# A ninth place for key rows, and turned value indices made one quarter earlier, in a one-core decoder layer with a product-key expert mixer

## Chip, cores and metric

One core of one Trainium2 chip. The metric is the device time of one launch in microseconds (us), the median of several runs. "Faster" and "slower" are against the kernel before, measured on the same chip.

## What is computed

One inference step of one decoder layer, for a prompt of 512 tokens and 8 sample tokens that share all parameters, model width 1024, everything in float32. The dense part is a recurrent branch beside a windowed attention branch, a gated merge and an output product. Then comes the expert mixer, and it is here that the change lies:

```python
def peer(h, w_pq, sub_keys, u_tab, v_tab):
    ...
    s = jnp.einsum('nhsd,hskd->nhsk', q.astype(jnp.float32), sub_keys.astype(jnp.float32))
    sv, si = lax.top_k(s, PEER_TOPK)
    cand = (sv[:, :, 0, :, None] + sv[:, :, 1, None, :]).reshape(n, PEER_HEADS, PEER_TOPK * PEER_TOPK)
    ...
    fv, fp = lax.top_k(cand, PEER_TOPK)
    ...
    def chunk(args):
        hc, ec, gc = args
        u = jnp.take(u_tab, ec, axis=0)
        act = jax.nn.gelu(jnp.einsum('cd,ced->ce', hc, u).astype(jnp.float32), approximate=False)
        wgt = (gc * act).astype(hc.dtype)
        vr = jnp.take(v_tab, ec, axis=0)
        return jnp.einsum('ce,ced->cd', wgt, vr)
```

Each token has 8 heads with 16 chosen experts each, so 128 rows of `u_tab` and 128 rows of `v_tab`, 4 KB each. A residual sum and a last norm follow.

## The kernel before

Five engines run programs of their own and meet at semaphores. The dense part goes in two chunks: tokens 0 to 255, then 256 to 511 with the 8 samples. It is a list of numbered products (`_plan`, `NO`), each with an estimated cost (`COST`), which TensorE works off in order into five PSUM buffers; the other engines follow its numbers.

The expert part of the first chunk can begin when its first scores are there (product 171, `PEER_FROM`), at about 383 us. From then on all engines interleave it with the rest of the dense list, step by step. A step is called a **quarter**. `MIDDLE[k]` and `LIMITS[k]` say how many dense products every engine has behind it in the middle and at the end of quarter k; the dense list is used up at quarter 140. There are 65 **groups** of 8 experts for 128 tokens (16 for each tile of 128 tokens, and group 48 for the 8 samples), so 520 slots on either side.

What a group goes through:

- **Key rows.** GpSimd gathers `u_tab` rows, one indirect DMA of 128 rows (512 KB) for each slot, two slots a quarter (`gather_u`, L2087; all gathers are recorded at L2085). Slot n goes to place n mod 8 of `u_row`. It waits for `s_idx` (the head's indices) and, from group 1 on, for `s_urd`, the dot that last read this place.
- **Dots.** VectorE multiplies the gathered row by the token's row and sums, one instruction (and the read of its sum) for each slot, two a quarter, two quarters behind (`dot_products`, L1910; the dot is L1924). Each lets `s_urd` go up.
- **Weights.** ScalarE makes gelu(dot) times the softmax share, in quarter 4g + 6 (`weights`, L1426; L1439, L1442).
- **Pack, turn and copy.** The value rows are wanted in another layout, 32 tokens for each row of partitions, so the indices and weights of a group have to be moved across partitions. VectorE packs them (`turn` on VectorE, L1993; L2000, waits for the group's weights `s_wcol`), TensorE turns them into the PSUM buffer `turned` (`turn` on TensorE, L1100; L1111, L1112, waits for `s_apart`), ScalarE copies the indices to `vidx` (L1460) and the weights to `spread` (L1461). `V_FROM[g]` is the quarter in which the first value row of group g is gathered. Before the change the pack stands in quarter `V_FROM[g] - 3`, the turn in `V_FROM[g] - 2` and the copy in `V_FROM[g] - 1`.
- **Value rows.** GpSimd gathers `v_tab` rows into the 8 places of `vt_row` (`gather_v`, L2100), between the key rows and in the same in-order queue. From quarter 11 to 127 these are three in two quarters, then some 2.4 a quarter (`V_AT`). A value gather waits for `s_vidx` and for the sums that last read its place (`s_vrd`). Groups 62 and 64 use the places of the key rows, since those are free at the end (`IN_U_PLACE`).
- **Sums.** TensorE multiplies `spread` by the value rows into the PSUM tensor `y`, four slots at a time, two quarters behind (`expert_sums`, L1115; L1128, 16 products). When a tile is complete the residual and the norm follow.

The order within a quarter on TensorE is: dense up to `MIDDLE`, the sums that are due, dense up to `LIMITS`, then a turn if one is due:

```python
                if k < len(LIMITS):
                    course.until(LIMITS[k])
                if k + TURN_LEAD - 1 in V_FROM and k + TURN_LEAD - 1 != V_FROM[SAMPLE_GROUP]:
                    turn(V_FROM.index(k + TURN_LEAD - 1))
```

Weights of the dense products come through SP's own DMA queue, and share the 16 DMA engines with the gathers.

## Time and profile before

| | us |
|---|---|
| median of 3 runs | 2036.07 |
| the runs | 2042.62, 2036.07, 2018.65 |
| the profiled execution | 2039.13 |
| its span | 2036.7 |
| busy: TensorE products, VectorE, ScalarE, GpSimd | 1348.9, 1282.7, 555.3, 1148.0 |
| moved by DMA | 701.81 MB, 545.33 of it by the gathers |

The profile is of one execution. In it a busy time is the sum over an engine's instructions. An idle time in brackets stands before the instruction named, with the one whose end let it go; a semaphore is counted by what raised it. "issue" means that the engine waited for nothing that the profile shows. Each row of a gather is the time in which GpSimd writes its descriptors; the transfer comes after it.

### The profile page before, as it was taken

The numbers are of one execution on the slowest core, as the hardware profiler recorded it, in microseconds if no ns is written. First come the engines' busy times: TensorE is split into PE (matmuls) and PEld (weight loads), VectorE is DVE, ScalarE is ACT, GpSimd is POOL, SyncE is SP. The second block draws the span as 40 slices with busy tenths as digits, with TensorE's granted clock in tenths as the row PEclk, the third lists the DMA queues.
The fourth block names the chain that finished last, engine by engine and source line by source line (L and its number), as shares of the span: only waits on it lengthen the run. The fifth ranks groups of instructions, "written<-read, shape, count | busy, mean of one in ns | idle before, by whom it ended". The sixth has DMA issues, their size and how long they took to land.

```text
span 2036.7 us, 23255 instructions
## 1 busy us (share of the span) xinstructions
PE 1348.9 (66%) x7318; PEld 870.6 (43%) x7318; DVE 1282.7 (63%) x3168; ACT 555.3 (27%) x1518; POOL 1148.0 (56%) x1062
## 2 busy tenths in 40 slices
PE   6998999748787787889878775343443344444344
PEld 5887899636555555666555442110111111111111
DVE  3265345577888888766767656566666556665640
ACT  2446423132354245112213222112112112211110
POOL 0100100356665556657666767777777777777774
PEclk9999999969889888879989887566666656666667
DMA  9755345799999988999999999999999999999997
GB/s 363 262 172 201 114 156 196 272 346 368 403 348 383 357 306 323 401 380 377 409 406 410 409 406 390 381 374 379 390 405 366 376 375 391 325 408 381 382 404 291
DMA packets 202440, 701.81 MB, mean 345 GB/s; under 512 B 22568, under 2 KB 32368, under 8 KB 202032
## 3 DMA queue, kind: packets, MB, share of 16 engines
q0 software_dynamic: 149760, 545.33, 69.3%
q1 hardware_dynamic: 52560, 155.02, 21.1%
q8 instruction: 59, 0.97, 0.2%
q14 instruction: 61, 0.50, 0.1%
HBM read 691.26 MB, written 11.06 MB: 345 GB/s over the span
## 4 chain that ended last, share of the span: by engine, by line
PE 25%; DMA 18%; issue 18%; DVE 17%; POOL 17%; ACT 3%; POOLq 0%; SPq 0%; DVEq 0%; ACTq 0%
POOL arena L2085 17%; DMA arena<-in_v_tab,pku 13%; PE acc L775 8%; DVE arena L1924 6%; PE y L1128 6%; DMA arena<-in_u_tab,pku 4%; PE acc L833 2%; PE acc L787 2%; PE acc L788 2%; PE acc L789 2%; ACT arena L1222 1%; DVE arena L1661 1%; PE acc L802 1%; DMA arena<-w_mod 1%; DVE pku L1945 1%
## 5 line engine op out<-in xcount | busy, mean ns | idle before, releaser
L1924 DVE CUSTOM_DVE_ANT_0 arena<-arena 128x1024 f32<-128x1024 f32 x520 | 627.2, 1223 | 368.7 <-DMA arena<-in_u_tab,pku 359.9
L2085 POOL DMA_INDIRECT arena<-in_u_tab,pku x520 | 567.4, 1091 | 400.3 <-issue 151.8
L1128 PE MATMUL y<-arena 128*32 128x512 f32 x2080 | 414.3, 909 | 548.3 <-DMA arena<-in_v_tab,pku 548.3
L2085 POOL DMA_INDIRECT arena<-in_v_tab,pku x520 | 565.5, 1088 | 232.3 <-issue 149.1
L775 PE MATMUL acc<-arena 128*128 128x264 f32 (+1 forms) x2304 | 544.0, 394 | 16.2 <-ACT arena L1238 7.6
L775 PEld LDWEIGHTS acc<-arena 128*128 128x128 f32 x2304 | 443.1, 195 | 120.9 <-issue 49.1
L1128 PEld LDWEIGHTS y<-arena 128*32 128x32 f32 x2080 | 82.4, 143 | 778.9 <-issue 768.7
L1460 ACT CAST pku<-turned 128x8 uint32<-128x8 f32 x64 | 10.2, 160 | 371.8 <-PE turned L1112 371.8
L1442 ACT ACTIVATE pk<-pk 128x1 f32<-128x1 f32 x520 | 103.5, 281 | 2.1
L1111 PE MATMUL turned<-arena 128*128 128x256 f32 x128 | 58.3, 547 | 59.3 <-DVE arena L2000 59.2
L2127 POOL TENSOR_TENSOR o_lo<-arena,o_hi 128x256 fp32r<-128x256 f32 x8 | 6.6, 866 | 156.7 <-ACT o_hi L1341 156.7
L1439 ACT ACT_TABLE_LOAD x37 | 47.5, 1283 | 157.9 <-issue 102.3
L1111 PEld LDWEIGHTS turned<-arena 128*128 128x128 f32 x128 | 26.6, 252 | 129.7 <-DVE arena L2000 64.7
L1439 ACT ACTIVATE pk<-pk 128x8 f32<-128x8 f32 x65 | 13.6, 209 | 198.0 <-DVE pk L1924 184.5
L1247 ACT ACTIVATE arena<-acc 128x256 f32<-128x256 f32 (+1 forms) x32 | 12.4, 386 | 152.6 <-PE acc L775 90.4
L833 PE MATMUL acc<-arena 128*128 128x256 f32 (+1 forms) x208 | 49.5, 396 | 5.6 <-DVE arena L1630 5.6
L1573 DVE SCALAR_TENSOR_TENSOR arena<-arena,par 128x256 f32<-128x256 f32 x60 | 29.1, 485 | 34.0 <-ACT arena L1281 32.6
L1741 DVE TENSOR_TENSOR w_lo<-arena,w_hi 128x1024 fp32r<-128x1024 f32 x32 | 39.1, 1228 | 14.4 <-ACT w_hi L1181 13.2
L1733 DVE SCALAR_TENSOR_TENSOR arena<-arena,acc 128x256 f32<-128x256 f32 (+1 forms) x16 | 6.8, 425 | 64.5 <-PE acc L775 64.5
L833 PEld LDWEIGHTS acc<-arena 128*128 128x128 f32 x208 | 39.9, 195 | 15.5 <-issue 9.5
L2117 POOL MEMSET arena<- 128x1536 f32 x2 | 2.8, 1388 | 76.6 <-DVEq L1784 76.6
L1222 ACT ACTIVATE arena<-arena,stat 128x256 f32<-128x256 f32 x64 | 31.7, 496 | 51.0 <-DVE stat L1667 51.0
(246 smaller groups left out, 1834.0 us busy)
## 6 DMA issues: line engine op xcount, KB each, us to landing
arena<-w_mod SPq DMA_DIRECT2D x48, 512.0 KB, 5.7
arena<-w_pq SPq DMA_DIRECT2D x32, 512.0 KB, 6.9
arena<-w_xr SPq DMA_DIRECT2D x20, 512.0 KB, 8.7
arena<-w_qk SPq DMA_DIRECT2D x20, 512.0 KB, 7.2
arena<-w_gr SPq DMA_DIRECT2D x20, 512.0 KB, 7.0
arena<-w_rnn SPq DMA_DIRECT2D x16, 640.0 KB, 6.3
arena<-in_u_tab,pku POOLq DMA_INDIRECT x520, 7.3
arena<-in_v_tab,pku POOLq DMA_INDIRECT x520, 6.7
```

The source lines that it names most:

```text
L775: mm = pe.matmul(a[:, 0:n], w[:, k, :], rhs[:, k, 0:n], start=(k == 0), stop=(k == ks - 1))
L787: pe.matmul(a[:, 0:CP], w1[:, k, :], hi[:, k, :], start=(k == 0), stop=False)
L788: pe.matmul(a[:, 0:CP], w1[:, k, :], lo[:, k, :], start=False, stop=False)
L789: mm = pe.matmul(a[:, 0:CP], w2[:, k, :], hi[:, k, :], start=False, stop=(k == DC - 1))
L833: mm = pe.matmul(a[:, 0:n], w[:, gate, i, :], xc[:, k, 0:n], start=(i == 0), stop=(i == len(BAND[j]) - 1))
L1111: pe.matmul(turned[:, 0:SLOT * 32], apart[n % 2][:, P:2 * P], to_rows, start=True, stop=True)
L1128: mm = pe.matmul(y[rows, h, :], spread[g % NTURN][:, 32 * j:32 * j + 32], rows_v[j][:, h * 512:(h + 1) * 512], start=first and (g != SAMPL ...
L1222: act.activation(probs[i % 2][:, j, :], probs[i % 2][:, j, :], ACT.Exp, bias=st[:, j:j + 1], accum_out=st[:, G + j:G + j + 1])
L1439: act.activation(gl, dots[g % 2], ACT.Gelu).then_inc(s_gl, 1)
L1442: ins = act.activation(wcol[at][:, j:j + 1], gl[:, j:j + 1], ACT.Copy, scale=gains[:, j:j + 1])
L1924: dve.tensor_tensor_reduce(u_row[j], u_row[j], h_of[o], 1.0, 0.0, ALU.mult, ALU.add, dots[g % 2][:, j:j + 1]).then_inc(s_urd, 1)
L2085: pool.indirect_dma_start(out=row, out_offset=None, in_=table, in_offset=bass.IndirectOffsetOnAxis(ap=idx, axis=0), **more).then_inc(signa ...
```

## The change

Two things.

The key rows get a ninth place. `u_row` and its semaphores `s_u` have 9 entries, slot n goes to place n mod 9, and a key gather waits for the dot of the ninth slot before it, no longer of the eighth. The areas behind it in the arena move by 4 KB for each partition. Value groups 62 and 64 still use key places 0 to 7, and count the fills of each by the new numbers.

`TURN_LEAD` goes from 3 to 4: the pack stands four quarters ahead of the group's first value gather, the turn three and the copy two.

```diff
+UPLACES = 9
...
-DOTS_LAG, TURN_LEAD, SUMS_LAG = 2, 3, 2
+DOTS_LAG, TURN_LEAD, SUMS_LAG = 2, 4, 2
...
+U_FILLS = [len(range(j, U_SLOTS, UPLACES)) for j in range(SLOT)]
+U_LAST = [range(j, U_SLOTS, UPLACES)[-1] for j in range(SLOT)]
...
-        u_row = [area(A_U + j * D, D) for j in range(SLOT)]
+        u_row = [area(A_U + j * D, D) for j in range(UPLACES)]
...
-                    pe.wait_ge(landed[j], 16 * V_NTH[g])
+                    pe.wait_ge(landed[j], 16 * (V_NTH[g] + (U_FILLS[j] if g in IN_U_PLACE else 0)))
...
-                    dve.wait_ge(s_u[j], 16 * (g + 1))
-                    dve.tensor_tensor_reduce(u_row[j], u_row[j], h_of[o], 1.0, 0.0, ALU.mult, ALU.add,
+                    nth, place = divmod(SLOT * g + j, UPLACES)
+                    dve.wait_ge(s_u[place], 16 * (nth + 1))
+                    dve.tensor_tensor_reduce(u_row[place], u_row[place], h_of[o], 1.0, 0.0, ALU.mult, ALU.add,
...
-                if g:
-                    pool.wait_ge(s_urd, SLOT * (g - 1) + j + 1)
+                n = SLOT * g + j
+                if n >= UPLACES:
+                    pool.wait_ge(s_urd, n - UPLACES + 1)
...
                 elif V_BEFORE[g] is None:
-                    pool.wait_ge(s_urd, SLOT * GROUPS + j + 1)
+                    pool.wait_ge(s_urd, U_LAST[j] + 1)
```

Line numbers of the changed kernel are 5 to 7 higher from here on (TensorE's products L775, L1111, L1112 and L1128 are L780, L1116, L1117 and L1133 there; VectorE's L1924 and L2000 are L1930 and L2006; GpSimd's L2085 is L2091).

GpSimd, the start of the gathers, with the semaphores waited for (`s_idx` indices of a head, `s_urd` dots, `s_ready` a dense product, `s_vidx` turned indices). Before:

```order
L2085 DMA arena<-in_u_tab,pku 128x1024 [waits s_idx]
L2085 DMA arena<-in_u_tab,pku 128x1024 x7
L2085 DMA arena<-in_u_tab,pku 128x1024 [waits s_idx,s_urd]
L2085 DMA arena<-in_u_tab,pku 128x1024 [waits s_urd] x7
L2085 DMA arena<-in_u_tab,pku 128x1024 [waits s_idx,s_urd]
L2085 DMA arena<-in_u_tab,pku 128x1024 [waits s_urd] x6
```
Changed:

```order
L2091 DMA arena<-in_u_tab,pku 128x1024 [waits s_idx]
L2091 DMA arena<-in_u_tab,pku 128x1024 x7
L2091 DMA arena<-in_u_tab,pku 128x1024 [waits s_idx]
L2091 DMA arena<-in_u_tab,pku 128x1024 [waits s_urd] x7
L2091 DMA arena<-in_u_tab,pku 128x1024 [waits s_idx,s_urd]
L2091 DMA arena<-in_u_tab,pku 128x1024 [waits s_urd] x6
```
The ninth gather waits no longer for a dot; the order is the same.

TensorE at the value rows that are first gathered in quarter 86 (group 14; `turned` is its turn, `y` the sums of others, `acc` dense products). Before:

```order
L1128 MATMUL y<-arena 32x512 x8
L775 MATMUL acc<-arena 128x264 x10
L915 MATMUL acc<-arena 64x2 x32
L917 MATMUL acc<-arena 64x64
L915 MATMUL acc<-arena 64x2 x32
L917 MATMUL acc<-arena 64x64
L775 MATMUL acc<-arena 128x264 x8
L1128 MATMUL y<-arena 32x512 x8
L1111 MATMUL turned<-arena 128x256
L1112 MATMUL turned<-arena 128x8
```
Changed:

```order
L1133 MATMUL y<-arena 32x512 x8
L780 MATMUL acc<-arena 128x264 x10
L920 MATMUL acc<-arena 64x2 x32
L922 MATMUL acc<-arena 64x64
L920 MATMUL acc<-arena 64x2 x32
L922 MATMUL acc<-arena 64x64
L1116 MATMUL turned<-arena 128x256
L1117 MATMUL turned<-arena 128x8
L780 MATMUL acc<-arena 128x264 x8
L1133 MATMUL y<-arena 32x512 x8
```
The turn stands ahead of 8 dense products and of a set of sums, behind which it stood before.

VectorE at the pack of the same group (L2000 before, L2006 in the changed one; MAX, MAX_INDEX and MATCH_REPLACE belong to the ranking of a later head, ISA is a dot). Before:

```order
L1952 TENSOR_TENSOR arena<-pk 128x256
L1956 MAX pk<-arena 128x8
L1957 MAX_INDEX pku<-pk,arena 128x8
L1959 MATCH_REPLACE arena<-pk,arena 128x256
L1956 MAX pk<-arena 128x8
L1957 MAX_INDEX pku<-pk,arena 128x8
L1960 TENSOR_SCALAR pk<-pk 128x1
L2000 TENSOR_TENSOR arena<-pk,arena 128x256
L1723 COPY arena<-acc 128x64
L1724 TENSOR_TENSOR arena<-arena,acc 128x64
L1726 COPY arena<-arena 128x8x8
L1924 ISA arena,pk<-arena 128x1024
```
Changed:

```order
L1953 MATCH_REPLACE arena<-pk,arena 128x128
L1950 MAX pk<-arena 128x8
L1951 MAX_INDEX pku<-pk,arena 128x8
L1954 CAST pk<-pku 128x32
L2006 TENSOR_TENSOR arena<-pk,arena 128x256
L1738 SCALAR_TENSOR_TENSOR arena<-arena,acc 128x264
L1930 ISA arena,pk<-arena 128x1024
L1930 ISA pk 128x1
L1930 ISA arena,pk<-arena 128x1024
L1930 ISA pk 128x1
L1958 TENSOR_TENSOR arena<-pk 128x256
L1962 MAX pk<-arena 128x8
```
The pack has moved ahead of a dense operation, two dots and the second ranking.

TensorE at the end of its program, the last turn. Before:

```order
L1112 MATMUL turned<-arena 128x8
L1128 MATMUL y<-arena 32x512 x16
L1111 MATMUL turned<-arena 128x256
L1112 MATMUL turned<-arena 128x8
L1128 MATMUL y<-arena 32x512 x16
L1111 MATMUL turned<-arena 128x256
L1112 MATMUL turned<-arena 128x8
L1128 MATMUL y<-arena 32x512 x32
```
Changed:

```order
L1117 MATMUL turned<-arena 128x8
L1133 MATMUL y<-arena 32x512 x16
L1116 MATMUL turned<-arena 128x256
L1117 MATMUL turned<-arena 128x8
L1133 MATMUL y<-arena 32x512 x16
L1116 MATMUL turned<-arena 128x256
L1117 MATMUL turned<-arena 128x8
L1133 MATMUL y<-arena 32x512 x40
```
The last turn has 8 more products of the sums behind it.

## Rows read from the trace of the kernel before

**Rows 1.** The page: busy share of the 16 DMA engines and rate, in 40 slices.

```profile
DMA  9755345799999988999999999999999999999997
GB/s 363 262 172 201 114 156 196 272 346 368 403 348 383 357 306 323 401 380 377 409 406 410 409 406 390 381 374 379 390 405 366 376 375 391 325 408 381 382 404 291
```

**Rows 2.** Busy time by stretch: us, each engine's busy us (instructions), PEclk, DMA share, GB/s.

```profile
400.00:820.00 420.00, 307.03 (x1412) 214.78 (x1416) 348.90 (x910) 161.63 (x441) 248.92 (x222) 0.85 0.94 355
820.00:1240.00 420.00, 341.33 (x1770) 239.83 (x1762) 286.73 (x719) 102.74 (x306) 277.93 (x251) 0.89 1.01 400
900.00:920.00 20.00, 20.00 (x131) 16.45 (x131) 8.88 (x25) 2.51 (x6) 6.25 (x7) 0.71 0.79 285
1250.00:1970.00 720.00, 299.21 (x1272) 83.05 (x1272) 439.66 (x1036) 124.44 (x419) 552.58 (x517) 0.61 0.99 381
```

**Rows 3.** Timeline, GpSimd: start, us, line, operation, idle before it and releaser.

```profile
383.01 1.09 POOL L2085 DMA_INDIRECT arena<-in_u_tab,pku  x1 [130.93 <-DVE pku L1983]
...
1453.75 1.27 POOL L2085 DMA_INDIRECT arena<-in_v_tab,pku  x1 [0.30 <-issue]
...
2018.10 0.94 POOL L2085 DMA_INDIRECT arena<-in_v_tab,pku  x1 [0.30 <-issue]
```

**Rows 4.** The page, costliest groups: the gathers of key and value rows.

```profile
L2085 POOL DMA_INDIRECT arena<-in_u_tab,pku x520 | 567.4, 1091 | 400.3 <-issue 151.8
L2085 POOL DMA_INDIRECT arena<-in_v_tab,pku x520 | 565.5, 1088 | 232.3 <-issue 149.1
```

**Rows 5.** Waits of GpSimd, 400 to 1250 us: us in total, times, longest.

```profile
POOL arena L2085 <- DVE pk L1924: 106.5, 37, 7.7
POOL arena L2085 <- PE y L1128: 38.5, 14, 7.7
POOL arena L2085 <- ACT pku L1460: 18.5, 5, 5.5
POOL arena L2085 <- DVE pku L1983: 13.2, 2, 7.1
```

**Rows 6.** Waits of GpSimd, 1250 to 1970 us.

```profile
POOL arena L2085 <- PE y L1128: 13.8, 17, 4.8
POOL arena L2085 <- ACT pku L1460: 2.7, 9, 0.3
POOL arena L2085 <- DVE pk L1924: 1.8, 1, 1.8
```

**Rows 7.** Timeline: GpSimd behind a dot, then TensorE behind value rows, twice.

```profile
570.39 1.61 POOL L2085 DMA_INDIRECT arena<-in_u_tab,pku  x1 [6.77 <-DVE pk L1924]
...
594.37 3.49 PE L1128 MATMUL y<-arena 128*32 128x512 f32 x16 [9.44 <-DMA arena<-in_v_tab,pku]
...
820.32 1.14 POOL L2085 DMA_INDIRECT arena<-in_u_tab,pku  x1 [2.50 <-DVE pk L1924]
...
838.90 3.64 PE L1128 MATMUL y<-arena 128*32 128x512 f32 x16 [4.34 <-DMA arena<-in_v_tab,pku]
```

**Rows 8.** Waits of TensorE for value rows: 400 to 820 us, then 820 to 1250 us.

```profile
PE y L1128 <- DMA arena<-in_v_tab,pku: 21.8, 4, 9.4
...
PE y L1128 <- DMA arena<-in_v_tab,pku: 76.2, 17, 9.9
```

**Rows 9.** Timeline, 901 to 918 us: pack, turn, and the gathers that waited.

```profile
901.77 0.42 DVE L2000 TENSOR_TENSOR arena<-pk,arena 128x256 f32<-128x256 f32 x1
...
910.41 1.14 POOL L2085 DMA_INDIRECT arena<-in_u_tab,pku  x1 [6.72 <-DVE pk L1924]
...
915.20 0.70 PE L1111 MATMUL turned<-arena 128*128 128x256 f32 x2
...
917.09 0.93 POOL L2085 DMA_INDIRECT arena<-in_v_tab,pku  x1 [5.54 <-ACT pku L1460]
```

**Rows 10.** Timeline, GpSimd, the last 50 us: gathers that waited for indices.

```profile
1998.47 0.94 POOL L2085 DMA_INDIRECT arena<-in_v_tab,pku  x1 [1.42 <-ACT pku L1460]
...
2009.39 0.94 POOL L2085 DMA_INDIRECT arena<-in_v_tab,pku  x1 [1.28 <-ACT pku L1460]
```

More of the change, by code:

```diff
@@ L320 @@
 V_BEFORE = [max([e for e in range(g) if (e in IN_U_PLACE) == (g in IN_U_PLACE)], default=None) for g in range(GROUPS + 1)]
-V_NTH = [sum(1 for e in range(g + 1) if (e in IN_U_PLACE) == (g in IN_U_PLACE)) + (GROUPS + 1 if g in IN_U_PLACE else 0) for g in range(GROUPS + 1)]
+V_NTH = [sum(1 for e in range(g + 1) if (e in IN_U_PLACE) == (g in IN_U_PLACE)) for g in range(GROUPS + 1)]
+U_FILLS = [len(range(j, U_SLOTS, UPLACES)) for j in range(SLOT)]
+U_LAST = [range(j, U_SLOTS, UPLACES)[-1] for j in range(SLOT)]
 A_H = 0
@@ L330 @@
 A_U = A_RING + OWN * SLOTW
-A_V = A_U + SLOT * D
+A_V = A_U + UPLACES * D
 A_HCUR = A_V + SLOT * D
@@ L502, in peer_program @@
         s_sidx, s_idxread = sem("s_sidx"), sem("s_idxread")
-        s_u = [sem(f"s_u{j}") for j in range(SLOT)]
+        s_u = [sem(f"s_u{j}") for j in range(UPLACES)]
         s_vt = [sem(f"s_vt{j}") for j in range(SLOT)]
@@ L2094, in gather_u @@
                         pool.wait_ge(s_idx, head + 1)
-                if g:
-                    pool.wait_ge(s_urd, SLOT * (g - 1) + j + 1)
+                n = SLOT * g + j
+                if n >= UPLACES:
+                    pool.wait_ge(s_urd, n - UPLACES + 1)
                 idx = eidx[head % NINDEX][:, part * SLOT + j:part * SLOT + j + 1] if g != SAMPLE_GROUP else eidx_s[:, j:j + 1]
-                gather(u_row[j], X["u_tab"], idx, s_u[j], {"engine_sem": s_idxread} if part and j == SLOT - 1 else {})
+                gather(u_row[n % UPLACES], X["u_tab"], idx, s_u[n % UPLACES], {"engine_sem": s_idxread} if part and j == SLOT - 1 else {})
             def gather_v(g, j):
```

## The prediction

> **What bounds the kernel now.** Read the 40 slices first [rows 1]. From the ninth slice on the DMA digit is 9 in all but three, so the first impression is a kernel held by its transfers. The rate row beside it says more: from there on the best slices stand at 401 to 410 GB/s, the others at 291 to 391. So 409 is about what the transfers can do here, and a slice below it is one in which less was asked for, or in which the asking was slow.
>
> The table by stretch [rows 2] divides the gathers' time. From 400 to 820 us VectorE is busy for 348.9 of 420 us (83%) and the rate is 355 GB/s: dense work on VectorE sets the pace. From 820 to 1240 us the rate is 400 GB/s and TensorE and the transfers set it together. From 1250 to 1970 us there is no dense work; VectorE is busy for 61% of it, TensorE for 42%, the rate is 381.
>
> Then GpSimd, which issues all 1040 gathers in one fixed order. A gather that meets nothing takes 0.94 us, with 0.30 us before it [rows 3]. From the first at 383.01 to the last at 2018.10 are 1635.1 us. At 1.24 us each, 1039 steps are 1288.4. The two groups of gathers are busy for 567.4 + 565.5 = 1132.9 us [rows 4], which is 155.3 over 1040 x 0.94. What is left, 1635.1 - 1288.4 - 155.3 = 191.4 us, is waiting. From 400 to 1250 us that is 106.5 us for dots (37 times), 38.5 for sums, 18.5 for turned indices, 13.2 for new indices [rows 5]. From 1250 to 1970 us only 1.8, 13.8 and 2.7 us are put down to dots, sums and indices, mostly the bare 0.30 [rows 6]. So the second half is an unbroken row of issues (517 gathers in 720 us, 1.39 us each), the first half is a chain of waits in which GpSimd stands before a full set of key places. The change works on the waits of the first half; the end moves only by as much as GpSimd reaches the second half earlier, and by what the last 50 us give.
>
> **The ninth place.** It removes no instruction and adds none: 520 dots, 520 key gathers, 520 value gathers as before, in the same order on GpSimd; only the dot waited for is the ninth before, not the eighth. Two dots fall in a quarter. Rows 2 have 222 + 251 = 473 gathers in 840 us, at mostly 3.5 a quarter, so a quarter is about 6.2 us and a dot comes every 3.1 us. The mean wait for a dot is 106.5 / 37 - 0.30 = 2.6 us. So one place more covers the average wait once. It does not cover it 37 times: where VectorE sets the pace, GpSimd runs one gather further ahead and then stands before the tenth. The sum of waits falls only as far as the pace itself gets quicker, or where a stretch of waiting is followed by one in which GpSimd or the transfers are late. So I do not book the 106.5 us. I book the places where TensorE waits for value rows that stood behind a GpSimd waiting for a dot. There are two clear ones before 850 us [rows 7]: GpSimd waits 6.77 us until 570.39 and TensorE then 9.44 us until 594.37; GpSimd waits 2.50 us until 820.32 and TensorE 4.34 until 838.90. The first value gather is also held by a value place, so I take 3 of its 6.5 us, and 2.2 of the other: 5 us. Below, nothing (VectorE is 83% busy there); above, the 21.8 us that TensorE waits for value rows in it [rows 8].
>
> **Indices one quarter earlier.** Each group's pack on VectorE, turn on TensorE and copy on ScalarE move by one quarter, in all 64 groups (the samples' group has only ScalarE's part); nothing is added. Their distance to each other stays one quarter, so where TensorE waits for a pack it comes to it a quarter earlier and is let go a quarter earlier, and I book nothing. What ends are GpSimd's waits for indices. The clearest is at 917.09 us, 5.54 us, right after one of 6.72 for a dot at 910.41; the turn that it waited for stood at 915.20 on TensorE behind a product and a sum set, although its pack was ready at 901.77 [rows 9]. With the turn in front of that product and that sum set, as the order shows, the indices are there before 910. In this hole the rate was 285 GB/s from 900 to 920 [rows 2]; at 409 those 20 us need 14, so the hole is worth 6.1 us, and both halves of the change work on it. I take 5; at least 0, at most 12.0 (both waits less 0.30 each). The waits of this kind left are in a queue already at 409 and I count them as nothing: the transfers there come when they come.
>
> In the last 50 us the case is plain. After the last key gather the value gathers follow at 1.24 us, and TensorE and ScalarE turn indices just in time: 1.42 us before 1998.47 and 1.28 before 2009.39 [rows 10], less 0.30 each, is 2.1 us, on the path that ends the run. Now the last turn stands 8 products earlier. The cover is the 8 places; I book all 2.1.
>
> **What it may cost.** The pack waits for its group's weights. For group 0 it had two quarters after them and has one; for later groups two or more. Behind it on VectorE stand dots, for which GpSimd and ScalarE wait. One such wait would be at most a quarter, 6 us, once; I take 0. The ninth place also puts a further 512 KB ahead of what SP and GpSimd ask for later, priced below as a rival.
> Gathers that no longer wait for the end of a dot will now issue beside one. Rows show what that is worth: the mean gather is 0.15 us over the bare 0.94, a single one among many dots 1.27 [rows 3, 4]; 37 x 0.15 = 6 us of GpSimd's time, in a stretch where it waits for some 160, so 0.
> On this the Trainium skill is harsher (SBUF — State Buffer, "SBUF: two separate sides"): a VectorE operation with two SBUF inputs and a GpSimd operation that reads SBUF exclude each other for the whole instruction. By that rule each of the 37 could lose a whole dot, and half the gain of the ninth place would go. The trace agrees in that long gathers are there at all and that the last one, when the dots have ended, takes 0.94 [rows 3]; it does not show a dot's whole length on average.
>
> **The sum.** 5 + 5 + 2.1 = 12.1 us. The profiled execution took 2039.1 (span 2036.7), 3.1 over the median of 2036.1 of the runs shown. 2039.1 - 12.1 = 2027.0, and against the median 2024.0.
>
> **Rivals.**
> First, the waits were a symptom. Where VectorE or the transfers set the pace, GpSimd merely changes the place at which it waits. For it: 83% VectorE, 400 GB/s in the second stretch, and from 1250 us on next to no waits for dots [rows 6], so that a further place has nothing to do there. Against it: the hole at 900. It leaves the tail's 2.1: 2034.
> The skill has a rule that would make this the only case (DMA: Bandwidth & Descriptors, "Specifications"): a core's limit to HBM is about 358 GB/s. By it the 381 and 400 GB/s of the stretches would be past the limit and no earlier gather could gain. The trace contradicts it with slices of 410, so it gets no more chance than the rows give.
> Second, the holes close. At 409 GB/s the bytes of the first stretch need 420 x 355/409 = 364.5 us, those of the second 410.8: 64.7 us below what they take. VectorE's 348.9 busy us would just allow it. But one place is one gather, and more than a third of that would surprise me: 22 + 2.1 = 24, so 2012.
> Third, slower. In the queue at 409 one more gather ahead is one more transfer of 512 KB, 1.28 us, before the value rows that TensorE waits for. From 820 to 1250 us TensorE waits for them 17 times, 76.2 us in all [rows 8]; 17 x 1.28 (524,288 bytes at 409 GB/s) = 22 us, if the dense products behind those waits carry it to the end. It decides if key rows are asked for before they are needed while value rows are late, which is what a place on the key side alone does. Against it: the number of gathers is the same, so the further one is ahead only once, and GpSimd asks for the value rows earlier as well. 2034 + 22 = 2056.
> That the change does not do what it says can only be in part: the order shows the ninth gather without its wait and the turns moved.
>
> **How the numbers follow.** Forecast 0.43 (2010 to 2031), symptom 0.25, holes closed 0.18, slower 0.14. A measurement of this kernel tells about 1% (20 us) from no change: faster by over 1% is below 2015.7, three quarters of the second rival and under a third of the forecast, 0.27; slower by over 1% is above 2056.4, half of the third and a little for the unforeseen, 0.10; the rest, 0.63, is within. Range 2004 to 2050: the holes closed somewhat better than priced, and most of the way to the slower case.
>
> **What would show it.** In the profile after: GpSimd's wait for turned indices from 400 to 1250 us down from 18.5 to under 5, and the two of the tail gone; its wait for dots down from 106.5 to 60 to 90, not to 0; the rate in the 20 us about 910 near 400; GpSimd's first gather of the unbroken row some 10 us earlier; the late stretch still 1.39 us a gather. The symptom case has the same counts but no earlier row. The slower case has TensorE's waits for value rows from 820 to 1250 us at 90 or more. I am wrong if waits for dots hardly fall, or if the late stretch's pace changes.

## The result and the profile after

The changed kernel takes 2045.2 us (median of 20 runs, 2031.65 to 2051.99) against 2038.19 us (20 runs, 2018.65 to 2046.97): a ratio of 1.0032, with a 95% interval from 1.0017 to 1.0046. It is slower by 0.3%, 6.5 us. That lies inside the 1% band and inside the range of the prediction, but the forecast was 12 us faster, so its sign was wrong. The profiled execution took 2042.17 us (span 2040.0), that of before 2039.13 (2036.7).

The page of the changed kernel has the groups of the two gathers [rows 4] and the group of the turns:

```profile
L2091 POOL DMA_INDIRECT arena<-in_u_tab,pku x520 | 572.6, 1101 | 369.9 <-issue 157.4
L2091 POOL DMA_INDIRECT arena<-in_v_tab,pku x520 | 562.1, 1081 | 264.4 <-issue 147.0
...
L1116 PE MATMUL turned<-arena 128*128 128x256 f32 x128 | 58.7, 549 | 86.5 <-DVE arena L2006 82.7
```

The page of the kernel before has for the last of these:

```profile
L1111 PE MATMUL turned<-arena 128*128 128x256 f32 x128 | 58.3, 547 | 59.3 <-DVE arena L2000 59.2
```

GpSimd stood less before key gathers (400.3 to 369.9 us) and more before value gathers (232.3 to 264.4). The sum is 1.7 us larger. On TensorE two rows grew: it stood 27 us longer before its turns, and its 2304 dense products of L775 (now L780) took 561.4 us in all, 544.0 before.

The stretches of the changed kernel, with the columns of [rows 2]:

```profile
400.00:820.00 420.00, 308.48 (x1393) 218.57 (x1393) 341.01 (x894) 159.48 (x436) 243.47 (x221) 0.83 0.92 349
820.00:1240.00 420.00, 346.12 (x1767) 244.28 (x1770) 287.92 (x718) 104.16 (x309) 277.83 (x249) 0.89 1.01 399
900.00:920.00 20.00, 20.00 (x161) 18.16 (x160) 11.53 (x32) 0.44 (x2) 8.61 (x9) 0.66 0.91 362
1250.00:1970.00 720.00, 301.05 (x1268) 82.56 (x1260) 442.71 (x1047) 124.91 (x419) 555.34 (x517) 0.63 1.00 382
```

In the first stretch VectorE, which sets the pace there, did 7.9 us less of its work in the same 420 us than before (341.01 against 348.90), at 349 instead of 355 GB/s. So the loss lies there. The hole at 900 closed for the most part (285 to 362 GB/s). The late stretch has the same 517 gathers in 720 us.

Its waits from 400 to 1250 us (waiting engine and line, what it waited for, us in total, times, longest; they answer to [rows 5]):

```profile
POOL arena L2091 <- DVE pk L1930: 85.1, 28, 9.7
PE turned L1116 <- DVE arena L2006: 81.8, 9, 26.5
POOL arena L2091 <- PE y L1133: 71.3, 20, 12.3
PE y L1133 <- DMA arena<-in_v_tab,pku: 68.1, 15, 9.8
POOL arena L2091 <- PE acc L780: 15.5, 2, 8.0
```

And two rows of the same list of the kernel before:

```profile
PE y L1128 <- DMA arena<-in_v_tab,pku: 98.0, 21, 9.9
PE turned L1111 <- DVE arena L2000: 59.2, 8, 26.4
```

GpSimd no longer waits for turned indices (18.5 us before), and waits 21 us less for dots. In exchange it waits for sums: 71.3 us and 15.5 put down to a product of TensorE, against 38.5. TensorE waits 30 us less for value rows and 22.6 us more for packs.

GpSimd's timeline, which has the two gathers of the tail that had waited [rows 10], and the last one [rows 3]:

```profile
1994.93 0.94 POOL L2091 DMA_INDIRECT arena<-in_v_tab,pku  x1 [0.30 <-ACT pku L1465]
...
2006.12 0.93 POOL L2091 DMA_INDIRECT arena<-in_v_tab,pku  x1 [0.30 <-ACT pku L1465]
...
2021.02 0.93 POOL L2091 DMA_INDIRECT arena<-in_v_tab,pku  x1 [0.30 <-issue]
```

The tail's 2.1 us came: both have only the bare 0.30.

**Where the time was lost.** Gathers have one fixed order, so the same gather can be looked up in each trace. The changed kernel is 2.8 us behind in quarter 16 (465 us), 6.6 in quarter 50 (683 us), 7.4 in quarter 139 (1237.10 before, 1244.52 after), 5.0 in quarter 257 and 2.9 at the last gather. Nearly everything is lost before 700 us, and three places where it happens can be read, at the turns of groups 0, 4 and 6. TensorE's timeline around the first group's turn, before:

```profile
424.30 1.22 PE L1111 MATMUL turned<-arena 128*128 128x256 f32 x2 [26.41 <-DVE arena L2000]
...
433.62 5.54 PE L812 MATMUL acc<-arena,const 128*128 128x264 f32 x16 [4.25 <-issue]
```

The same place in the changed kernel:

```profile
421.20 1.22 PE L1116 MATMUL turned<-arena 128*128 128x256 f32 x2 [26.55 <-DVE arena L2006]
...
435.57 6.35 PE L817 MATMUL acc<-arena,const 128*128 128x264 f32 x16 [4.43 <-issue]
```

The turn comes 3.1 us earlier, yet TensorE stands in front of it as long as before, because work that used to run ahead of it now stands behind it, and the dense products (L812, now L817) begin 2.0 us later and take 0.8 us longer. VectorE, which waits for ScalarE's L1188 and through it for these very products, stands longer and goes on 2.8 us later, as much as GpSimd is behind in quarter 16. Before:

```profile
439.71 1.80 DVE L1548 RECIPROCAL arena<-arena 128x264 f32<-128x264 f32 x1 [9.65 <-ACT arena L1188]
```

After:

```profile
442.48 1.80 DVE L1553 RECIPROCAL arena<-arena 128x264 f32<-128x264 f32 x1 [12.78 <-ACT arena L1193]
```

The second place is the turn of group 4. Before:

```profile
549.67 3.62 PE L849 MATMUL acc<-arena 128*128 128x256 f32 x16
559.24 1.22 PE L1111 MATMUL turned<-arena 128*128 128x256 f32 x2 [5.95 <-DVE arena L2000]
```

After:

```profile
545.50 3.83 PE L780 MATMUL acc<-arena 128*128 128x264 f32 x16
560.73 1.22 PE L1116 MATMUL turned<-arena 128*128 128x256 f32 x2 [11.39 <-DVE arena L2006]
...
562.03 6.28 PE L780 MATMUL acc<-arena 128*128 128x264 f32 x16
```

Products that had run before the turn now stand behind it, and TensorE stands 11.39 us instead of 5.95. On VectorE's timeline the pack stood 4.4 us behind the cast of new indices before:

```profile
554.38 0.17 DVE L1983 CAST pku<-pk 128x16 uint32<-128x16 f32 x1
...
558.77 0.42 DVE L2000 TENSOR_TENSOR arena<-pk,arena 128x256 f32<-128x256 f32 x1
```

and stands directly behind it after the change:

```profile
560.16 0.17 DVE L1989 CAST pku<-pk 128x16 uint32<-128x16 f32 x1
560.25 0.43 DVE L2006 TENSOR_TENSOR arena<-pk,arena 128x256 f32<-128x256 f32 x1
```

The pack did move ahead in VectorE's order. But VectorE comes to the same cast 5.8 us later, so the pack is no earlier in time, while the turn that waits for it stands a quarter earlier in TensorE's order. The two stretches 549 to 561 and 562 to 568 us have in the kernel before (columns of [rows 2])

```profile
549.00:561.00 12.00, 6.05 (x28) 4.79 (x30) 10.57 (x26) 2.04 (x5) 8.63 (x7) 0.82 1.03 395
562.00:568.00 6.00, 6.00 (x31) 3.41 (x24) 4.19 (x16) 2.09 (x8) 1.32 (x2) 0.88 0.85 298
```

and in the changed one

```profile
549.00:561.00 12.00, 0.60 (x3) 0.28 (x2) 11.29 (x31) 1.47 (x5) 6.74 (x7) 0.68 1.01 393
562.00:568.00 6.00, 6.00 (x17) 4.74 (x18) 3.83 (x9) 2.91 (x10) 2.86 (x3) 0.58 0.72 221
```

In the changed kernel TensorE stood for all but 0.60 of the first 12 us, and in the 6 us of the second row the granted clock is 0.58, near the lower of its two levels (1.2 of 2.4 GHz), against 0.88 before: 16 products of L780 took 6.28 us where 16 had taken 3.83 at 545.50.

The third place is the turn of group 6. GpSimd's first gather of quarter 40 (617 us) is still 2.3 us ahead of the kernel before, that of quarter 44 is 8.1 behind. About half of this step, 5.3 us, is in e1 below too, which has the ninth place alone; the rest comes only with the earlier turn. Before:

```profile
628.80 0.70 PE L1111 MATMUL turned<-arena 128*128 128x256 f32 x2
...
632.32 1.92 PE L1128 MATMUL y<-arena 128*32 128x512 f32 x16
```

After:

```profile
630.15 1.19 PE L1116 MATMUL turned<-arena 128*128 128x256 f32 x2 [3.84 <-issue]
...
631.43 8.83 PE L838 MATMUL acc<-arena 128*128 128x264 f32 x30
...
640.19 1.93 PE L1133 MATMUL y<-arena 128*32 128x512 f32 x16
```

The profile names no releaser for the 3.84 us, but the pack ran from 629.63 to 630.05, right before the turn (from 628.32 before). Of the 26 products of L833 (now L838) that ran ahead of this turn, 18 now stand behind it, and the set of sums behind them comes 7.9 us later. A value gather at 642.98 then waits 3.83 us for it.

### The profile page after: what moved, and what is told of

It is laid out like the page before. It is cut to its first block, busy times and chain, and to the rows that moved or that the text cites. A ratio compares the mean times of both kernels' runs of the same rounds, so it can differ in the third digit from the quotient of the medians.

```text
span 2040.0 us, 23255 instructions
## 1 busy us (share of the span) xinstructions
PE 1358.2 (67%) x7318; PEld 879.2 (43%) x7318; DVE 1282.2 (63%) x3168; ACT 556.0 (27%) x1518; POOL 1149.8 (56%) x1062
## 4 chain that ended last, share of the span: by engine, by line
POOL 16%; issue 15%; DMA 13%; PE 11%; DVE 3%; POOLq 0%; ACT 0%; ACTq 0%; DVEq 0%; SPq 0%
POOL arena L2091 16%; DMA arena<-in_v_tab,pku 11%; PE y L1133 5%; PE acc L780 5%; DMA arena<-in_u_tab,pku 1%; DVE arena L1930 1%; PE acc L920 1%; PE turned L1116 0%; POOLq L2087 0%; DMA key_rows<-arena 0%; DMA arena<-key_rows 0%; DVE pku L1951 0%; PE acc L904 0%; PE acc L817 0%; DVE pk L1950 0%
## 5 line engine op out<-in xcount | busy, mean ns | idle before, releaser
L1930 DVE CUSTOM_DVE_ANT_0 arena<-arena 128x1024 f32<-128x1024 f32 x520 | 627.1, 1223 | 368.1 <-DMA arena<-in_u_tab,pku 361.6
L2091 POOL DMA_INDIRECT arena<-in_u_tab,pku x520 | 572.6, 1101 | 369.9 <-issue 157.4
L1133 PE MATMUL y<-arena 128*32 128x512 f32 x2080 | 408.9, 899 | 514.1 <-DMA arena<-in_v_tab,pku 514.1
L2091 POOL DMA_INDIRECT arena<-in_v_tab,pku x520 | 562.1, 1081 | 264.4 <-issue 147.0
L780 PE MATMUL acc<-arena 128*128 128x264 f32 (+1 forms) x2304 | 561.4, 402 | 20.5 <-ACT arena L1243 12.4
L780 PEld LDWEIGHTS acc<-arena 128*128 128x128 f32 x2304 | 454.1, 200 | 131.7 <-issue 53.9
L1133 PEld LDWEIGHTS y<-arena 128*32 128x32 f32 x2080 | 80.9, 141 | 746.7 <-issue 746.0
L1116 PE MATMUL turned<-arena 128*128 128x256 f32 x128 | 58.7, 549 | 86.5 <-DVE arena L2006 82.7
L1116 PEld LDWEIGHTS turned<-arena 128*128 128x128 f32 x128 | 27.1, 256 | 152.6 <-DVE arena L2006 93.7
L838 PE MATMUL acc<-arena 128*128 128x256 f32 (+1 forms) x208 | 51.1, 407 | 4.4 <-DVE arena L1635 4.4
L838 PEld LDWEIGHTS acc<-arena 128*128 128x128 f32 x208 | 41.5, 202 | 14.0 <-issue 7.4
L1950 DVE MAX8 pk<-arena 128x8 f32<-128x128 f32 x132 | 38.7, 293 | 11.7 <-ACT arena L1387 7.5
```

Of the source, the lines that this page charges most:

```text
L780: mm = pe.matmul(a[:, 0:n], w[:, k, :], rhs[:, k, 0:n], start=(k == 0), stop=(k == ks - 1))
L838: mm = pe.matmul(a[:, 0:n], w[:, gate, i, :], xc[:, k, 0:n], start=(i == 0), stop=(i == len(BAND[j]) - 1))
L1116: pe.matmul(turned[:, 0:SLOT * 32], apart[n % 2][:, P:2 * P], to_rows, start=True, stop=True)
L1133: mm = pe.matmul(y[rows, h, :], spread[g % NTURN][:, 32 * j:32 * j + 32], rows_v[j][:, h * 512:(h + 1) * 512], start=first and (g != SAMPL ...
L1930: dve.tensor_tensor_reduce(u_row[place], u_row[place], h_of[o], 1.0, 0.0, ALU.mult, ALU.add, dots[g % 2][:, j:j + 1]).then_inc(s_urd, 1)
L1950: rank(dve.max(b, x))
```

## The experiments

Ratios are against the kernel before on the same chip, each with its 95% interval. No kernel leaves out any work. Ratios of runs on different chips are compared by way of each one's own kernel before. The theories at the start were: the earlier turn stands before a pack that is not earlier (A), or the ninth place itself costs, by a further key gather ahead of value rows (B). "Ninth place" in a diff stands for the parts of the change about UPLACES.

**The change taken apart.** e1 is the ninth place alone, with the leads of before:

```diff
 (changed kernel)
-DOTS_LAG, TURN_LEAD, SUMS_LAG = 2, 4, 2
+DOTS_LAG, TURN_LEAD, SUMS_LAG = 2, 3, 2
```

> The ninth place alone, indices packed, turned and copied three, two and one quarter ahead as before. Theory A (the earlier turns cost the time: TensorE waited 81.8 us for packs from 400 to 1250 us, before 59.2, and dense products that filled that wait now come after it): this kernel does not have the cost, so 0 to -5 us against before, and TensorE's wait for packs near 59 us. Theory B (the ninth place costs it: GpSimd runs a key row further ahead and then stands before value places, 71.3 us instead of 38.5, and value rows come later): +4 to +9 us, and GpSimd's wait for sums near 70 us.

Measured: 0.998 [0.9955, 1.0006]. B would have shown itself here and did not. The waits of 400 to 1250 us in e1:

```profile
POOL arena L2091 <- DVE pk L1930: 70.1, 22, 8.9
PE turned L1116 <- DVE arena L2006: 63.0, 9, 25.8
POOL arena L2091 <- PE y L1133: 52.9, 20, 7.0
POOL arena L2091 <- ACT pku L1465: 25.3, 4, 13.7
```

The waits for dots fall from 106.5 to 70.1; those for sums rise from 38.5 to 52.9 and those for indices from 18.5 to 25.3, so over half of what the place removes returns elsewhere by these rows. Counted over GpSimd's single gathers, with the bare 0.30 us taken off each, nearly all of it returns: its waits of 400 to 1250 us are 170.8 us before and 166.7 in e1. Ahead of key gathers they fall from 111.5 to 61.9, ahead of value gathers they rise from 59.4 to 104.8. The gather of quarter 139 starts 2.4 us earlier.

e2 is the other half alone, eight places and the longer leads:

```diff
 (kernel before)
-DOTS_LAG, TURN_LEAD, SUMS_LAG = 2, 3, 2
+DOTS_LAG, TURN_LEAD, SUMS_LAG = 2, 4, 2
```

> Eight places, indices one quarter earlier. Theory A: +5 to +9 us against before, TensorE's wait for packs from 400 to 1250 us near 80 us, GpSimd's gather of quarter 139 some 7 us later than before. Theory B: within 2 us of before, GpSimd's wait for sums near 38 us. Both: the two waits for indices in the last 50 us gone, about 2 us.

Measured: 1.0047 [1.0021, 1.0073], the gather of quarter 139 8.8 us late. The row of its waits that matters:

```profile
PE turned L1111 <- DVE arena L2000: 84.0, 10, 27.1
```

The whole loss is in this half, and with it TensorE's longer standing before packs (59.2 to 84.0). Without the ninth place the three steps are plainer: GpSimd's first gather is 2.3 us late in quarter 28, 6.5 in quarter 36 (behind group 4) and 11.5 in quarter 44 (behind group 6).

e3 moves only VectorE's pack a quarter earlier, with turn and copy as before and eight places:

```diff
 (kernel before)
-                if k + TURN_LEAD in V_FROM and k + TURN_LEAD != V_FROM[SAMPLE_GROUP]:
-                    turn(V_FROM.index(k + TURN_LEAD))
+                if k + TURN_LEAD + 1 in V_FROM and k + TURN_LEAD + 1 != V_FROM[SAMPLE_GROUP]:
+                    turn(V_FROM.index(k + TURN_LEAD + 1))
```

> Eight places; only VectorE's pack goes one quarter earlier, turn and copy stay where they were before. If what costs is that TensorE stands before a pack, this takes most of the 59 us of such waits away at no price: theory A expects -3 to -10 us against before and TensorE's wait for packs from 400 to 1250 us under 25 us. If the dense stretch is held by VectorE anyway (TensorE's wait only a symptom), 0, with the wait gone all the same and turned up at other products. Theory B has no opinion: 0.

Measured: 0.9983 [0.9955, 1.0011], which by the times alone can't be told from no change. TensorE's waits for packs nearly halve (the row below; under 25 us was expected), and its turn of group 4 no longer waits:

```profile
PE turned L1111 <- DVE arena L2000: 34.0, 3, 23.2
```

Its gather of quarter 139 is 7.8 us earlier than before. That is the gain that the change could have had in the first half. Its medians show only a part of it; the last gather of the profiled execution was 6.6 us later, because its late stretch was slow (the profiled execution, 2044.75 us, was the longest of its 12). That stretch in e3 has 506 gathers (373 GB/s) against 517, with an unchanged order there but for the pack. e11 below has 509 with no edit to the order at all, so this pace differs between executions and is not put down to the pack.

e4 has nine places, and all three steps earlier only for groups whose value rows begin in quarter 150 or later (from about 1300 us on):

```diff
 (changed kernel, TURN_LEAD back to 3)
+LEAD = [TURN_LEAD + int(V_FROM[g] >= 150) for g in range(GROUPS + 1)]
+PACK_AT = [V_FROM[g] - LEAD[g] for g in range(GROUPS + 1)]
...
-                if k + TURN_LEAD - 1 in V_FROM and k + TURN_LEAD - 1 != V_FROM[SAMPLE_GROUP]:
-                    turn(V_FROM.index(k + TURN_LEAD - 1))
+                if k - 1 in PACK_AT and k - 1 != PACK_AT[SAMPLE_GROUP]:
+                    turn(PACK_AT.index(k - 1))
```

> Nine places; the earlier pack, turn and copy only for groups whose value rows begin at quarter 150 or later, when the dense work is over. Theory A: the tail's 2 us without the cost of the first half, so -2 to -7 us against before. Theory B: +2 to +7 us.

Measured: 0.9972 [0.9946, 0.9997]. With the early groups left alone the loss is gone. What the later groups' leads add to e1 can't be told from no change.

**Where and why the lead costs.** What was open after this: whether it is the standing before the pack, or only that dense products come behind the turn (A2). The next three have nine places and lists of their own for the three steps:

```diff
 (changed kernel, TURN_LEAD back to 3)
+PACK_AT = [V_FROM[g] - (5 if g else 4) for g in range(GROUPS + 1)]
+TURN_AT = [V_FROM[g] - (3) for g in range(GROUPS + 1)]
+COPY_AT = [V_FROM[g] - (2) for g in range(GROUPS + 1)]
...
+                if k in TURN_AT and k != TURN_AT[SAMPLE_GROUP]:
+                    turn(TURN_AT.index(k))
```

That is e5: turn and copy where the changed kernel has them, the pack a quarter further ahead.

> The changed kernel (nine places, turn three and copy two quarters ahead) with the pack five quarters ahead instead of four (group 0: four). It leaves the turn where the change put it and takes TensorE's standing before the pack away. Theory A1 (the cost is the standing: the pack is not ready at the turn's earlier place): -3 to -9 us against before, TensorE's wait for packs from 400 to 1250 us under 45 us instead of 81.8. Theory A2 (the cost is that dense products come after the turn, whatever it waits for): still +1 to +5 us, with the wait gone.

Measured: 0.9991 [0.9963, 1.0018]. Its wait row, and the turn of group 4 on its TensorE timeline:

```profile
PE turned L1119 <- DVE arena L2009: 30.5, 4, 26.9
```

```profile
550.70 0.70 PE L1119 MATMUL turned<-arena 128*128 128x256 f32 x2 [1.68 <-DVE arena L2009]
...
551.37 3.81 PE L783 MATMUL acc<-arena 128*128 128x264 f32 x16
```

The dense products stand behind the turn as in the changed kernel, but the turn waits 1.68 us instead of 11.39, and the 16 products behind it take 3.81 us instead of 6.28. In quarter 139 this kernel is 3.7 us ahead of the one before, and one with the pack at four quarters (e6) 6.8 behind. So the standing costs, not the order alone, and A2 falls. Group 0, whose pack could not go further ahead, still shows its 2.2 us in quarter 16. Its time is 1.8 us below the kernel before, a miss between the two theories' ranges (3 to 9 us faster, 1 to 5 slower), and its interval and that of the changed kernel (from 1.0017) just touch. But e5 and e6 ran on the same chip, with medians of 2040.02 and 2045.09 us; their means differ by 7.2 us, give or take 4.2, so the times say the same as the traces.

e6 has the changed kernel's leads only for the groups before quarter 150, the mirror image of e4:

```diff
+PACK_AT = [V_FROM[g] - (4 if V_FROM[g] < 150 else 3) for g in range(GROUPS + 1)]
+TURN_AT = [V_FROM[g] - (3 if V_FROM[g] < 150 else 2) for g in range(GROUPS + 1)]
+COPY_AT = [V_FROM[g] - (2 if V_FROM[g] < 150 else 1) for g in range(GROUPS + 1)]
```

> The complement of the kernel with the late groups alone: nine places, pack, turn and copy a quarter earlier only for groups whose value rows begin before quarter 150. Both A1 and A2 put the whole cost of the change here: +5 to +9 us against before, TensorE's wait for packs near 80 us, the two waits of the last 50 us back. A theory that the earlier turns cost throughout, in the late stretch too, expects half of it, +2 to +4 us.

Measured: 1.0038 [1.0012, 1.0064], waits for packs 81.9 us, quarter 50 6.7 us late, as in the changed kernel. Against e1 (0.998) the early leads alone cost 0.58%, 12 us give or take 7, and the two intervals do not meet.

e7 has nine places, the early pack of e3 everywhere, and turn and copy earlier only from quarter 150 on:

```diff
+PACK_AT = [V_FROM[g] - (4) for g in range(GROUPS + 1)]
+TURN_AT = [V_FROM[g] - (2 if V_FROM[g] < 150 else 3) for g in range(GROUPS + 1)]
+COPY_AT = [V_FROM[g] - (1 if V_FROM[g] < 150 else 2) for g in range(GROUPS + 1)]
```

> A version to beat both: nine places; before quarter 150 only the pack a quarter earlier, turn and copy as in the kernel before; from quarter 150 on all three a quarter earlier as in the change. If the gains of the parts add (ninth place -4, pack alone -4, tail -2): -7 to -12 us against before. If ninth place and earlier pack fill the same hole: -3 to -6 us.

Measured: 0.9988 [0.9961, 1.0016]: a miss. Its waits for packs fall to 35.4 us as meant, but it is 2.4 us below the kernel before, where 3 to 12 was expected, and not faster than e1 or e4. The gains did not add up.

**The ninth place on the other side.** In e1 GpSimd moves from waiting for key places to waiting for value places. So e8 gives the ninth place to value rows: 8 key places, 9 value places, leads as before. Of its diff the core:

```diff
+UPLACES = 8
+VPLACES = 9
...
+V_SLOT = {(g, j): SLOT * i + j for i, g in enumerate(V_GROUPS) for j in range(SLOT)}
...
+A_HCUR = A_V + VPLACES * D
...
-                    pool.wait_ge(s_vrd, 2 * V_BEFORE[g] + j // QUAD + 1)
+                    e, i = V_AT_SLOT[m - VPLACES]
+                    pool.wait_ge(s_vrd, 2 * e + i // QUAD + 1)
```

> Eight key places and the ninth place on the value side (value slot m goes to place m mod 9 and waits for the sums that read slot m - 9), leads as before. GpSimd's waits for sums were 38.5 us in before and 52.9 with nine key places, so if value places are what the key place ran into, this takes 20 to 30 us of those waits and gives -2 to -6 us. If the transfers at 409 GB/s hold that stretch, within 2 us of before. Cost theory B (a further place only crowds the transfers) expects +2 to +6 us.

Measured: 0.9946 [0.9919, 0.9973], 11 us faster where 2 to 6 was expected. The waits of 400 to 1250 us:

```profile
POOL arena L2099 <- issue: 164.8, 433, 6.4
...
POOL arena L2099 <- DVE pk L1938: 115.6, 38, 7.0
...
POOL arena L2099 <- PE y L1141: 14.4, 6, 4.0
...
POOL arena L2099 <- ACT pku L1473: 3.6, 1, 3.6
```

The waits for sums fall from 38.5 to 14.4 us and those for turned indices from 18.5 to 3.6; the ones for dots rise only by 9. But the waits for which the profile shows no releaser rise too, from 139.4 us (420 times) to 164.8 (433 times), some 21 us more than 13 further bare waits of 0.30. Counted over the single gathers as for e1, the waits are 165.8 us in all (170.8 before, 166.7 in e1): ahead of value gathers 32.2 instead of 59.4, ahead of key gathers 133.6 instead of 111.5. So the waiting moves here too, the other way. In quarter 139 e8 is 2.5 us ahead, no more than e1 with its 2.4. What it gained beyond e1 lies behind that, where a single execution does not settle it.

Value places come free four at a time (TensorE sums four rows in a set), key places one with each dot. That might make a ninth place worth more on this side; it was not tested, and the traces of the first half do not bear it out.

e9 adds the earlier pack, turn and copy from quarter 150 on; e10 moves, besides, the pack earlier everywhere:

```diff
 (e9, on e8)
+PACK_AT = [V_FROM[g] - (3 if V_FROM[g] < 150 else 4) for g in range(GROUPS + 1)]
+TURN_AT = [V_FROM[g] - (2 if V_FROM[g] < 150 else 3) for g in range(GROUPS + 1)]
+COPY_AT = [V_FROM[g] - (1 if V_FROM[g] < 150 else 2) for g in range(GROUPS + 1)]
 (e10: the first of them)
-PACK_AT = [V_FROM[g] - (3 if V_FROM[g] < 150 else 4) for g in range(GROUPS + 1)]
+PACK_AT = [V_FROM[g] - (4) for g in range(GROUPS + 1)]
```

> Eight key places, nine value places, and pack, turn and copy a quarter earlier only for groups whose value rows begin at quarter 150 or later. Nine value places gave 0.9946; the tail's waits for indices are worth at most 2 us more. If the gains add: -10 to -15 us against before. If the 0.9946 was partly chance, -5 to -9 us.

> The same with the pack alone a quarter earlier before quarter 150. If taking TensorE's standing before packs away is a gain of its own (3.5 us in the median when done alone, 7 us at quarter 139): -13 to -18 us. If, as beside the ninth key place, the two fill the same hole or the late stretch gives it back: -6 to -12 us, and GpSimd's mean gather from 1250 to 1970 us 20 to 50 ns longer than before.

Measured: e9 0.9937 [0.9918, 0.9956], e10 0.9926 [0.9899, 0.9954] with a median of 2026.81 us, the fastest of all here and 0.7% below the kernel before. The three intervals of e8, e9 and e10 overlap, so what the two additions bring is not told from nothing. That a ninth value place is worth more than a ninth key place shows when kernels with equal leads are paired: e8 against e1 (0.9946, 0.998), e9 against e4 (0.9937, 0.9972), e10 against e7 (0.9926, 0.9988). All three differ the same way, by 0.3 to 0.6%, and in the last pair the intervals do not meet. e8 and e7, which ran on one chip, differ in their means by 7.1 us, give or take 4.6. Waits of e10:

```profile
PE turned L1125 <- DVE arena L2017: 32.4, 4, 22.8
...
POOL arena L2102 <- PE y L1144: 7.4, 6, 4.9
```

A ninth place on both sides at once was not measured.

e11 asks whether the addresses, not the place, make e8 faster: the kernel before with 4 KB left empty behind the value places.

```diff
 (kernel before)
-A_HCUR = A_V + SLOT * D
+A_HCUR = A_V + SLOT * D + D
```

> The kernel before with 4 KB left empty behind the value places, so that everything behind them lies where it lies with nine value places; no place is added. If the gain of the ninth value place is the place: within 2 us of before, GpSimd's waits for sums from 400 to 1250 us near 38 us. If it is the addresses: -5 us or more.

Measured: 1.0011 [0.9986, 1.0035]. Addresses are not it. Its trace also tells how far two executions of one order lie apart: 0.8 us in quarter 139, but 9.0 us at the last gather. Its late stretch:

```profile
1250.00:1970.00 720.00, 290.63 (x1256) 79.71 (x1256) 436.48 (x1031) 122.33 (x411) 557.65 (x509) 0.63 0.99 376
```

## Why the prediction went wrong

**The distance between pack and turn: the step that failed.** The text had: "Their distance to each other stays one quarter, so where TensorE waits for a pack it comes to it a quarter earlier and is let go a quarter earlier, and I book nothing." The first half is right, the second is not. The distance in the order stays; the pack's time does not move with its place in the order. It was 3.1 us earlier for group 0, and 1.5 us later for group 4 (558.77 to 560.25). VectorE is the engine that is late in this stretch, and part of its work waits for dense products that TensorE and ScalarE bring forth. These products now stand behind a turn that waits for VectorE. So TensorE stands longer (59.2 to 81.8 us), VectorE's next inputs come later, and the products themselves run at a lower granted clock after the standing. The runs show each link. From 400 to 820 us VectorE's waits for ScalarE, summed over its wait rows, are 41.2 us before, 42.0 in e1 and 41.5 in e5, but 51.1 in the changed kernel, 49.3 in e2 and 50.5 in e6. The 2304 dense products take 544.0, 545.0 and 553.3 us in the first three and 561.4, 563.2 and 561.2 in the others. e6 against e1 puts the price at about 12 us; e5 shows that with the pack ready it goes. How much of it is the order and how much the clock was not separated. The rows were there: a turn that waits 26.41 and 5.95 us for a pack says that TensorE arrives too early, and moving it still earlier could only help if the pack's engine had time to spare, which the 83% of [rows 2] denied.

**The ninth place, -5.** Of the right size: e1's 0.998 is -4.1 us, with an interval from -9 to +1, so it is not told from nothing. The gather of quarter 139 starts 2.4 us earlier, and 5.6 in e4, whose order is the same up to there. The reason given, that the place covers a wait only where GpSimd is late elsewhere, holds; what was not seen is the place to which the waiting moves, the value places.

**The hole at 900, -5.** It closed (285 to 362 GB/s; "near 400" was too much), but the chain was 6.6 us late ahead of it and 7.4 behind it, so it brought nothing that can be seen at the end. A rate in a 20 us stretch was taken for time on the path. Nor did both halves work on it: with the leads alone (e2) those 20 us ran at 398 GB/s, with the ninth place alone (e1) at 273. The turn came at 913.77 us, not before 910. The text's upper bound of 12.0 should read 11.7 (6.72 + 5.54 - 0.60).

**The tail, -2.1.** Right: both waits are at the bare 0.30. From quarter 257 to the last gather the changed kernel makes up 2.1 us (5.0 to 2.9). In time, e4 against e1 puts the leads of the late groups at -1.6 us, with some 7 us of uncertainty, where 2.1 was booked. What the hole gave is inside the 12 us of e6 against e1, with the opposite sign.

**The sum.** By the experiments: -4.1 - 1.6 + 12 = +6, and 6.5 was measured; by the prediction -12.1. The sum of the experiments is uncertain by some 9 us, so that it comes so near is partly luck.

**Longer gathers beside dots, 0.** Fair: key gathers went from 1091 to 1101 ns, value gathers from 1088 to 1081. The reason is below: a gather loses only what is left of the dot that runs when it begins, not the whole dot.

**The pack behind its weights, 0.** For this reason nothing was lost; the wait sat on the other side, with the turn.

**The marks.** Waits for dots 60 to 90: 85.1, right. Waits for indices under 5: none, right. Late stretch 1.39 us a gather: right. Gathers 10 us earlier at the end of the first half: 7.4 later, wrong. The slower rival named another mechanism and a mark for it, TensorE's waits for value rows of 90 us or more from 820 to 1250 us; they fell from 76.2 to 58.6 us, so its sign was right and its reason wrong. Neither of the text's two signs of being wrong came (waits for dots that hardly fall, another pace of the late stretch); it had no mark for TensorE's waits for packs, the row that grew. The first rival, that GpSimd merely changes the place at which it waits, describes the ninth key place best.

## What to carry to other kernels

Before an instruction is moved ahead on an in-order engine, look at what it waits for: if it stands there already, moving it and its producer by the same number of steps lengthens the wait, unless the producer's engine has time to spare. Move the producer first, alone, and read whether the wait goes (59.2 to 34.0 us here). And before a buffer gets one more place, ask where the issuing engine will stand next: the place brought 0.2% (an interval that includes no change) on the side with the larger sum of waits (106.5 us for dots) and 0.5% (clear of no change) on the side with the smaller (38.5 us for sums); why it brought more there stays open. A wait for the engine that sets the pace only moves elsewhere.

## What the runs showed of the hardware

After TensorE had stood for 11.4 us, its granted clock was 0.58 over the next 6 us, and 16 products took 6.28 us where 16 of the same shape took 3.83 before the standing. A wait of this engine thus costs more than its length.

The late stretch, whose order e11 leaves as it is, ran with 509 to 517 gathers in 720 us in two executions of the same order (376 and 381 GB/s), 9 us at the last gather, while the same two lay 0.8 us apart at 1237 us. Other pairs with one order up to quarter 139 lay 0.6 (changed kernel and e6), 1.3 (e8 and e9) and 3.2 us (e1 and e4) apart there. Where a kernel ends in such a stretch, one profile each does not settle 10 us; the position of one gather ahead of it does, but it does not settle 3 us.

Counted over the single rows of the kernel before from 1250 us on, of 75 gathers with no VectorE work beside them none took over 1.1 us, and of 408 that met a dot 105 did. Which ones these are can be read from when they began. 166 gathers began with 0.14 us or more left of a running dot, and 164 of them ended 0.80 to 0.82 us after that dot's end, so the longest took 1.99 us. The gather at 1453.75 [rows 3] is one: the dot ran from 1452.99 to 1454.21, and the gather ended at 1455.02. The other way round there is no such wait: of 144 dots that began 0.15 to 0.9 us after a gather had begun beside no dot, every one took its usual 1.2 us, and 140 of these gathers took no more than 0.96. So a gather is held until the running dot is over, while a dot that begins 0.15 us or more into a gather neither is held nor holds it. The Trainium skill (SBUF — State Buffer, "SBUF: two separate sides") lets such a pair exclude each other for the whole instruction; the trace agrees where the dot began first (164 of 166) and not where the gather did.
